# Attention heads: ScalarE's copy of the turned probabilities is moved ahead of the next unit's exponential, and the first two key tiles are loaded and divided in four pieces each

## The reference, cut to what matters

```python
mn = rmsnorm(mem, mem_norm_g[l])
kv = (mn @ w_mem_kv[l]).reshape(b, mem.shape[1], 2, N_MEM_HEADS, MEM_HEAD_DIM)
...
scores = jnp.einsum('bcqhd,bckhd->bhcqk', qc, kb).astype(jnp.float32) * (hd ** -0.5)
scores = scores + bias[None, :, None, :, :]
scores = jnp.where(valid[None, None, :, None, :], scores, NEG_INF)
p = jax.nn.softmax(scores, axis=-1).astype(v.dtype)
out = jnp.einsum('bhcqk,bckhd->bcqhd', p, vb)
```

## Time and profile before

| | |
|---|---|
| median of 3 runs | 2950.72 us (2949.64 to 2961.76) |
| the profiled execution | 2947.98 us, of which its span 2946.2 us |
| mean granted clock of TensorE in it | 0.989 |
| PE busy | 2877.6 us, 98% of the span |
| DVE busy | 2168.8 us, 74% |
| ACT busy | 1503.5 us, 51% |
| POOL busy | 158.3 us, 5% |

### The profile page before, as it was taken

One profiled execution on the slowest core, in us unless ns is written; L12 is line 12 of the kernel. 1 busy time (PEld: TensorE's weight loads), 2 busy tenths in 40 slices (PEclk: granted clock), 3 DMA queues, 4 the chain that ended last, 5 costly groups with the idle time before them and its releaser, 6 DMA issues.

```text
span 2946.2 us, 45953 instructions
## 1 busy us (share of the span) xinstructions
PE 2877.6 (98%) x18068; PEld 2596.4 (88%) x18068; DVE 2168.8 (74%) x2666; ACT 1503.5 (51%) x1709; POOL 158.3 (5%) x228
## 2 busy tenths in 40 slices
PE   9999999999999999999999999999999999999998
PEld 8888788888888899999999989988989889889887
DVE  5644459999875999999999874555755875875874
ACT  5544554445554544444444454545544664664763
POOL 3000000000000000000000110111010000000001
PEclk9999999999999999999999989999999999999999
DMA  7545445555553988888878655444316885885981
GB/s 279 186 157 183 167 144 186 189 191 187 201 205 140 361 332 333 319 329 331 321 308 325 253 195 200 164 153 156 132 52 230 332 332 222 330 317 215 355 315 72
DMA packets 114815, 692.26 MB, mean 235 GB/s; under 512 B 14144, under 2 KB 27696, under 8 KB 33648
## 3 DMA queue, kind: packets, MB, share of 16 engines
q1 hardware_dynamic: 109088, 675.33, 61.0%
q10 hardware_dynamic: 4688, 11.01, 1.2%
q0 software_dynamic: 896, 3.93, 0.4%
HBM read 679.74 MB, written 10.49 MB: 234 GB/s over the span
## 4 chain that ended last, share of the span: by engine, by line
PE 83%; DVE 7%; ACT 6%; issue 3%; DMA 1%; POOL 0%; SPq 0%; DVEq 0%; ACTq 0%; POOLq 0%
PE psT L1197 21%; PE psT L1198 11%; PE psT L1184 5%; PE psT L1186 5%; PE psT L1185 5%; PE psT L1765 3%; PE psT L1767 3%; PE psT L1766 3%; PE psT L1306 3%; ACT w_hi L594 2%; PE psT L1754 2%; PE psT L1756 2%; PE psT L1755 2%; DVE w_lo L1881 2%; PE psY L1805 1%
## 5 line engine op out<-in xcount | busy, mean ns | idle before, releaser
L1881 DVE TENSOR_TENSOR w_lo<-raw,w_hi 128x2048 fp32r<-128x2048 f32 x534 | 1224.4, 2296 | 394.2 <-ACT w_hi L594 390.5
L594 ACT ACTIVATE w_hi<-raw 128x2048 fp32r<-128x2048 f32 x534 | 1019.2, 1910 | 396.6 <-PE psT L1186 135.9
L1197 PE MATMUL psT<-a_both,w_hi 128*128 128x512 f32 x3072 | 1086.3, 398 | 8.6 <-DVE a_both L1931 2.8
L1198 PE MATMUL psT<-a_both,w_lo 128*128 128x256 f32 x3072 | 860.0, 280 | 0.0
L1197 PEld LDWEIGHTS psT<-a_both,w_hi 128*128 128x128 f32 x3072 | 578.3, 188 | 148.6 <-issue 8.9
L1198 PEld LDWEIGHTS psT<-a_both,w_lo 128*128 128x128 f32 x3072 | 581.0, 189 | 0.3
L1184 PE MATMUL psT<-a_both,w_hi 128*128 128x256 f32 x784 | 229.5, 293 | 6.8 <-DVE w_lo L1881 4.4
L1184 PE MATMUL psT<-h_hi,w_hi 128*128 128x256 f32 (+1 forms) x800 | 228.6, 286 | 2.9 <-DVE h_lo L2257 1.7
L1186 PE MATMUL psT<-h_hi,w_lo 128*128 128x256 f32 (+1 forms) x800 | 227.4, 284 | 0.0
L1185 PE MATMUL psT<-h_lo,w_hi 128*128 128x256 f32 (+1 forms) x800 | 227.3, 284 | 0.0
L1186 PE MATMUL psT<-a_both,w_lo 128*128 128x256 f32 x784 | 224.5, 286 | 0.0
(11 more groups left out here) (367 smaller groups left out, 4561.4 us busy)
## 6 DMA issues: line engine op xcount, KB each, us to landing
raw<-tiles_dram SPq DMA_DIRECT2D x534, 1024.0 KB, 5.3
pool<-ada_tiles_dram SPq DMA_DIRECT2D x96, 1024.0 KB, 5.1
bias_rows_dram<-pool ACTq DMA_DIRECT2D x1, 8192.0 KB, 52.7
pool<-bias_rows_dram SPq DMA_DIRECT2D x40, 128.0 KB, 4.4
pool<-bias_rows_dram SPq DMA_DIRECT2D x40, 64.0 KB, 4.6
pool<-mem_dram SPq DMA_DIRECT2D x4, 512.0 KB, 10.5
pool<-x_dram ACTq DMA_DIRECT2D x1, 2048.0 KB, 12.1
pool<-x_dram POOLq DMA_DIRECT2D x1, 2048.0 KB, 9.9
```

The source lines that it names most:

```text
L594: nc.scalar.activation(w_hi[:, t.k % SPL, :], raw[:, t.k % RAW, :], ACT.Copy).then_inc(hi_done, 1)
L1197: nc.tensor.matmul(dst.rearrange("p (h s) -> p h s", h=2), wh, a_both[:, :, a, :], start=first, stop=False)
L1198: return nc.tensor.matmul(dst[:, 0:S], wl, a_hi[:, a, :], start=False, stop=last)
L1881: nc.vector.tensor_tensor(w_lo[:, t.k % SPL, :], raw[:, t.k % RAW, :], w_hi[:, t.k % SPL, :].bitcast(F32), ALU.subtract).then_inc(lo_done, 1)
```

## The change

In `attend` on ACT, the copy of unit u-3 now stands ahead of the exponential of unit u. Its waits are the same: for the transposes of unit u-3 and for the products of unit u-5. At the start, tile 0 is loaded in four pieces of 128x512 that alternate with the four quarters of the memory input, tile 1 in four pieces after them; ACT and DVE divide piece by piece, and PE waits for a piece before every fourth chunk. It runs 24 products on ones ahead of them in place of 30.

```diff
-            for g in range(4):
-                sp.dma_start(chunks(MEMX + 4 * g, 4), mem_d[:, 4 * g:4 * g + 4, :]).then_inc(L[f"mem{g}"], 16)
-                if g == 0:
-                    load_tile(Tile(0))
-            for k in range(1, 4):
+            def load_piece(k, p):
+
+                sp.dma_start(raw[:, k, 512 * p:512 * p + 512], tiles[k, :, 512 * p:512 * p + 512])\
+                    .then_inc(pieces_landed[k][p], 16)
+
+            for g in range(4):
+                sp.dma_start(chunks(MEMX + 4 * g, 4), mem_d[:, 4 * g:4 * g + 4, :]).then_inc(L[f"mem{g}"], 16)
+                load_piece(0, g)
+            for p in range(4):
+                load_piece(1, p)
+            for k in range(2, 4):
                 load_tile(Tile(k))
...
             def attend(units, at, scratch, ticks=None):
                 n = len(units)
                 for u in range(n + 3) if ticks is None else ticks:
+                    if u >= 3:
+                        v = u - 3
+                        unit, slot = units[v], (at + v) % 2
+                        act.wait_ge(W["probs_transposed"], at + v + 1)
+                        wait(act, W["pv_ready"], at + v - 1)
+                        dst = flat(scratch[1] + 2 * slot, 2)
+                        w = {"mem": 2 * S, "cmp": S}.get(unit["kind"], S + P)
+                        ins = nc.scalar.activation(dst[:, 0:w], psP[:, 0:w], ACT.Copy)
+                        ins.then_inc(W["probs_copied"], 1)
                     if u < n:
                         unit, slot = units[u], (at + u) % 2
                         act.wait_ge(W["max_ready"], at + u + 1)
...
                         last.then_inc(W["exp_ready"], 1)
-                    if u >= 3:
-                        v = u - 3
...
+            def piece_hi(k, p):
+
+                act.wait_ge(pieces_landed[k][p], 16)
+                nc.scalar.activation(w_hi[:, k, 512 * p:512 * p + 512], raw[:, k, 512 * p:512 * p + 512], ACT.Copy)\
+                    .then_inc(W["first_hi"] if p < 3 else hi_done, 1)
+
             for g in range(4):
                 act.wait_ge(L[f"mem{g}"], 16)
                 mem_hi(g)
-                if g == 0:
-                    split(Tile(0))
-            split(Tile(1))
+                piece_hi(0, g)
+            for p in range(4):
+                piece_hi(1, p)
...
-            idle_products(30)
-            feature_major(Tile(BASE["km"]), "mem")
-            feature_major(Tile(BASE["km"] + 1))
+            idle_products(24)
+            for k in range(2):
+                for c in range(DC):
+                    if c % 4 == 0:
+                        if c < 12:
+                            pe.wait_ge(W["first_lo"], 3 * k + c // 4 + 1)
+                        else:
+                            pe.wait_ge(lo_done, k + 1)
+                    chunk_split(None if k else "mem", c)
+                    last = three(psT[:, k, 0:S], Tile(k), a_hi[:, c, :], a_lo[:, c, :], c, c == 0, c == DC - 1)
+                last.then_inc(used, 1)
...
-            mem_lo(0)
-            lo(Tile(0))
-            for g in range(1, 4):
+            def piece_lo(k, p):
+
+                if p < 3:
+                    dve.wait_ge(W["first_hi"], 3 * k + p + 1)
+                else:
+                    dve.wait_ge(hi_done, k + 1)
+                at = 512 * p
+                nc.vector.tensor_tensor(w_lo[:, k, at:at + 512], raw[:, k, at:at + 512],
+                                        w_hi[:, k, at:at + 512].bitcast(F32), ALU.subtract)\
+                    .then_inc(W["first_lo"] if p < 3 else lo_done, 1)
+
+            for g in range(4):
                 mem_lo(g)
-            lo(Tile(1))
+                piece_lo(0, g)
+            for p in range(4):
+                piece_lo(1, p)
```

More of the change, by code:

```diff
@@ L395, in build @@
                  "gain_last_squares", "gain_sums", "rstd_ready", "normed_pairs", "tail_chunk",
-                 "carried", "pre_ready", "rstd_columns", "rstd_columns_copied", "conv_lane", "centred_lane"]
+                 "carried", "pre_ready", "rstd_columns", "rstd_columns_copied", "conv_lane", "centred_lane", "first_hi", "first_lo"]
         W = {n: sem(n) for n in names}
+        pieces_landed = [[sem(f"first_piece{k}_{p}") for p in range(4)] for k in range(2)]
         bias_landed = [sem(f"bias_landed{i}") for i in range(2)]
@@ L592, in split @@
                 wait(act, used, (t + -SPL).count())
-                act.wait_ge(landed[t.k % RAW], t.plus(16 * (t.k // RAW + 1), 16 * (t.n // RAW)))
+                act.wait_ge(landed[t.k % RAW], t.plus(16 * (t.k // RAW + (t.k % RAW > 1)), 16 * (t.n // RAW)))
                 nc.scalar.activation(w_hi[:, t.k % SPL, :], raw[:, t.k % RAW, :], ACT.Copy).then_inc(hi_done, 1)
```

## The result

The changed kernel takes 2939.11 us (median of 6 executions, 2934.67 to 2942.46); the kernel before, now with 6 executions, 2956.87 us (2949.64 to 2961.76). The ratio is 0.9945 [0.993, 0.996]: the kernel is faster by 0.4 to 0.7%, some 16 us. The forecast was 2932 with a range of 2925 to 2942. The profiled executions differ by less, 2947.98 against 2942.46 us. That of before was a lucky one, 8.9 us under its median: in the 41 further executions of the kernel before that the experiments brought, none took under 2948.92, and the medians were 2953.36 to 2955.80. That of the changed kernel was the slowest of its six, 3.4 us over its median.

The account below looks back on a forecast made before the run. PE, busy 2877.6 of 2946.2 us, bounds the kernel, its largest wait being for ACT's copy. Gains 9.5 + 6.5 + 2.8 = 18.8 us off 2947.98 give 2929.2, as a median 2932; range 2925 to 2942.

Parts of the forecast that it names:

- Local attention: First block's local attention: copy hidden in ACT's wait for maxima, 8.1 us direct plus 1.4 from the clock, 9.5 us.
- the residual of 0.9 us: End of local attention: of 9.0 us of PE's waits for the copy, about 0.9 stays as PE outruns the loop.
- rival A: PE's waits move to DVE's or POOL's next product; local attention about 5.5, second block 3, start 2: 2940 us; chance 0.20.
- The estimate of the loop: Local attention: the ACT-DVE loop shortens by 4 x 0.37 = 1.5 us per 34 us round, to 32.5; PE needs 31.8.
- The clock's 1.4 us: End of local attention, 412 to 420 us: low clock after the longest wait costs up to 1.7 us, 1.4 returned.
- Second block: Second block's attention: 4.2 us from waits for the copy plus 2.3 from waits for POOL, 6.5 us.
- The start: Loading and division in pieces: PE begins tile 1 at 19.1 instead of 22.02, gain 2.8 us, bounds 0 and 4.
- A low clock inside tile 0 is hidden by the gaps: Start: low clock costs nothing in tile 0, up to 1.6 us in tile 1; 0.1 us charged.
- Later: After the start: tile 4's load waits for tile 0's remainder, 17.65 instead of 13.9; cost nothing, without the queue up to 3.7.
- B: The start gives nothing, through landings or a low clock in tile 1: gain 16 us, 2935 us; chance 0.12.
- C: Attention: each copy delays the exponential it precedes, 0.37 us a unit, at worst 25 us slower, 2976 us; chance 0.03.
- D: Attention: the new order changes nothing because PE's waits are really POOL's; only the start gains, 2948 us; chance 0.05.

Follow-up runs that it names:

- the repeat: The changed kernel, unaltered, profiled and timed again on one chip beside other kernels: 2937.84 us, ratio 0.9942 to the kernel before.
- the key sums first: Changed kernel, but DVE copies the first four key tiles' sums out of PSUM before the remainder three tiles ahead: 2935.9 us, ratio 0.994; again 2933.86, 0.9928.
- part 1 alone: Kernel before with only ACT's copy moved ahead of the exponential, start unchanged: 2940.37 us, ratio 0.9944; again 2935.78, 0.9934.
- two banks: Changed kernel with the key sums first, plus every second local head's product with the values in another PSUM bank: 2933.16 us, ratio 0.9927.

## Why the prediction was right, and where it was not

The time fell into the range, and the gain of 18.8 us stands beside 16.3 by the ratio. Step by step the agreement is partly luck: two terms were too large or of the wrong sign, one too small.

**The base.** "That execution lies 2.7 us under the median", of three executions. With six it lies 8.9 under it, and 5.4 to 7.8 under the three later medians. The median of before alone moved by 6.2 of the 7.1 us by which 2932 fell short.

**Local attention, 9.5 forecast, 4.7 and 6.3 measured.** The copy is hidden in the wait for the maxima, as the step said, and all six waits for it went. What the step left out is what PE needs two instructions on: the residual of 0.9 us became 5.2 (5.1 in the repeat), at DVE's copy-out, which the text named for the second block only. This is the mechanism of rival A, with A's own figure for this stage (5.5). The estimate of the loop was not far off: 16 units are some three rounds, 4.5 to 4.8 us by the text, and from the first score to the last the stage shortened by 4.0 and 3.9. With a second bank behind the copy-out the stage gave 9.3, so the 9.5 were there to be had in the stage, but not by this change. The clock's 1.4 us did not return in the first profile (0.79) and did in the second (1.00 at 412 to 420).

**Second block, 6.5 forecast, 8.5 and 10.0 measured.** Right in mechanism, small in size. (Against the second profile of before, 435.2 us, it would be 11.9 and 13.4, so the size is known to some 3 us only.) The text left 0.6 of 4.8 for the copy and 1.6 of 3.9 for POOL; all went, and only 0.8 came back, at DVE's copy-out at L1681 (1.3 before, 2.1 after). For POOL's seven waits it had counted one copy, 0.37 us, off each; that more than this came off each of the longer ones, 0.8 at most, is measured, and why was not tested. The windows show the outcome, 1880 to 1910 us, in before and in the changed kernel (the block's bias rows start at 1677.8 and 1678.4):

```profile
1880.00:1910.00 30.00, 29.22 (x232) 28.43 (x231) 17.05 (x56) 14.97 (x32) 4.23 (x10) 1.00 0.40 134
```
```profile
1880.00:1910.00 30.00, 30.00 (x240) 29.29 (x239) 18.11 (x64) 16.16 (x36) 4.23 (x10) 1.00 0.43 149
```

**The start, 2.8 gain forecast, 1.5 to 5.2 loss measured: the step that failed.** Four statements of it were wrong. The first is that the second quarter lands at about 8.6: ACT got it at 10.20 and 10.77. In 4 to 6 us whole tiles had moved 368 GB/s in before and 366 with whole loads in the changed kernel; the pieces moved 157:

```profile
4.00:6.00 2.00, 2.00 (x12) 2.00 (x11) 0.00 (x0) 0.40 (x1) 0.59 (x2) 1.00 0.78 157
```

An estimate from the windows: 1.25 MB had been moved by 6.6 us in before and by 8.2 in the changed kernel, 1.6 later, and the quarter landed 1.6 later than 8.6. The prediction had named the bound, half the rate for the small rows, and not taken it. That the short rows are the cause is not shown: the order of transfers changed with them, and whole tiles and quarters moved only 187 GB/s in 6 to 8 us in before. The Trainium skill, "DMA: Bandwidth & Descriptors", section "Bandwidth", advises transfers of 1 MiB or more. The 157 GB/s in 4 to 6 us agree with it; the 362 GB/s in 8 to 10, still with pieces, do not. PE nevertheless began the second tile near 20.6 (its 49th product), where 22.02 was and 19.1 was forecast; in the repeat it began at 21.9 only.

The second is "A low clock inside tile 0 is hidden by the gaps". The remainder of tile 0's last piece was there at about 18.5 and 19.1 in the two profiles, and the last 12 products, 1.4 us at full speed, ended at about 20.6 and 21.9. With the clock at 0.50 a burst lasted as long as the next piece took, and nearly no gap was left; that cost some 0.7 and 1.4 us. In the first profile with the key sums first, where the clock stayed at 1.00, PE began the second tile at 19.87. The third: the text counted five issues where six stood ahead of tile 2 and expected it out at about 8; it went out at 10.07, and ACT waited 0.54 and 0.77 us for tiles 2 and 3, which were put at nothing.

The fourth, which cost the time, stands under "Later" and puts what follows at nothing. The text looked at what waits for tile 0's data place, not at what waits for its place in PSUM. PE's third tile needs DVE's copy of the first one's sums, DVE makes it behind the remainder of the fourth tile, and ACT reaches the fourth tile at 24.97 and 24.37 in place of 23.25: three pieces of tile 0 now stand behind the second quarter, and in the first profile ACT waited 1.3 us for the late tiles. In the kernel before the copy came at 27.41, just when the second tile ended. So as long as DVE's copy stayed behind a fourth tile that ACT divides no earlier, nothing done to tiles 0 and 1 could have gained. With the copy moved ahead, the pieces gained 2.4, 2.2 and 1.5 us at the start in three profiles, near the 2.8.

**The signs named.** The wait for L739 was to fall to about 1 and POOL's under 2; both fell to nothing. Copies stand ahead of exponentials that still wait, as named. The clock of 412 to 420 was at 1.00 in one profile of two. PE began the second tile at 20.6 and 21.9, not near 19. Signs of being wrong were to be quarters after 12 and 14 us (ACT took the third at 12.70 and the fourth at 15.19 without waiting) and new entries at the transposes (there are none). The list watched L1399 and the scores, and the new waits came at two lines that it did not watch.

**Rivals.** A was right for local attention and wrong for the second block. B (the start gives nothing) was too mild. C did not occur: ACT's copy waited for the transposes 2.1 us in three waits in the whole local stage (1.5 in one before). D fell with both wait entries.

**What stays open.** Why executions of one kernel differ by up to 14 us. Two places are seen in the traces: the second block's heads, 431.8 us in one profile of before and 435.2 in the other with nearly the same waits (from 1700 to 1730 us the clock was 1.00 in one, 0.89 in the other), and ACT's waits for tiles in the expert part, 62.4 us in one profile of the changed kernel and 24.7 in the other.

## What to carry to other kernels

A wait that is removed is worth what the next wait on that engine leaves of it; list every resource the freed engine asks for in the same tick (each single PSUM buffer, and who empties it, behind what) before taking the sum. When work is moved or cut at one place of an in-order list, follow every later entry of that list to its reader, the small copies above all. In the local stage a second buffer helped by 3 us where an earlier copy hurt by 2, because the earlier copy stood ahead of the maxima that the exponential waits for.

## What the hardware showed that was not expected

- PE, never idle and at a clock of 1.00, runs the same loop of products at two rates: 1386 and 1387 matmuls in 440 to 680 us in before and in the changed kernel, 1360 in part 1 alone, in its repeat and with two banks; the mean 128x512 product shows 394 or 399 ns (before, then two banks, 440 to 680 us):

```profile
L1197 PE MATMUL psT<-a_both,w_hi 128*128 128x512 f32 x693 | 240.3, 394 | 0.0
```
```profile
L1210 PE MATMUL psT<-a_both,w_hi 128*128 128x512 f32 x680 | 240.3, 399 | 0.0
```

  Over the gates that is 5.0 us. Eight profiles show the faster rate and six the slower. Four kernels were profiled twice, and each kept its rate, so it seems to go with the program and not with the execution. What in the program sets it stays open, as does whether it can be chosen; by an estimate two banks at the faster rate would be some 5 us better still. Whether the executions without a profile keep the rate isn't known, so a comparison of times between kernels of different rate is unsure by these 5 us.
- An issue on SP takes 0.42 us at first and 2.2 to 3.2 for the sixth transfer in five of six profiles with pieces (in the sixth the one before it took 1.91 and it 1.22). In the changed kernel less than the first transfer, 512 KB, had been moved when that issue began at 3.44 (16 GB/s in 0 to 2 us, 251 in 2 to 4). A quarter of the memory took 8.2 us from issue to landing in the median.
- A low clock does not always follow a wait: 3.95 us of waiting for the third tile were followed by 0.50 for six microseconds, 1.5 us in the repeat were not; but waits of 2.90 and 3.08 us before the second burst of the first tile were followed by 0.50 in one profile and by 1.00 in the other.
